# A two-layer decoder step on one core: the second feed-forward network computed by seven block products in place of eight

## The reference

```
x += 0.5 * SwiGLU_a(rms(x))
h = rms(x); p = h @ W_in;  x += W_out [ RWKV7(p_rw) | mLSTM(p_ml) | NSA(p_nsa) ]
x += MemXAttn(rms(x), mem)          # 4 heads, 256 memory tokens
x += 0.5 * SwiGLU_b(rms(x))         # D_FF = 2816

def _swiglu(h, w_up, w_down):
    gate, up = jnp.split(h @ w_up, 2, axis=-1)
    return (jax.nn.silu(gate) * up) @ w_down
```

## Time and profile before

| | us |
|---|---|
| device time, median of 3 runs | 3831.72 |
| lowest and highest of the 3 | 3829.81, 3835.63 |
| span of the profiled execution | 3827.4 |
| PE busy in it | 3565.6 (93%) |
| DVE, ACT, POOL busy | 1295.4, 564.3, 180.2 |

### The profile page before, as it was taken

The page is one execution under the profiler, slowest core; times in us unless marked ns, Lnnn a source line. Parts: engine busy times, 40 slices in busy tenths (PEclk is TensorE's granted clock), DMA queues, the critical chain, the costliest instruction groups (busy, mean ns, idle before and its releaser), DMA issues. The chain is left out here.

```text
span 3827.4 us, 44331 instructions
## 1 busy us (share of the span) xinstructions
PE 3565.6 (93%) x18084; PEld 2313.9 (60%) x18084; DVE 1295.4 (34%) x3074; ACT 564.3 (15%) x1261; POOL 180.2 (5%) x282
## 2 busy tenths in 40 slices
PE   7999899999999999997987968988899999999998
PEld 4666565666567777665665734444565556656776
DVE  3445603223312223314543458743432122111111
ACT  1000011000011101012223426630110001000000
POOL 3111100000000000000001100000000000000000
PEclk8999999999999999997687869999999999999999
DMA  6565554232234332335335431031043342233443
GB/s 158 178 190 169 169 143 117 87 97 75 88 111 118 102 98 71 101 121 112 43 82 157 141 99 55 7 124 39 12 124 91 96 119 80 76 98 110 124 128 91
DMA packets 607237, 401.76 MB, mean 105 GB/s; under 512 B 90636, under 2 KB 584060, under 8 KB 602556
## 3 DMA queue, kind: packets, MB, share of 16 engines
q1 hardware_dynamic: 578956, 314.10, 30.0%
q0 software_dynamic: 13824, 67.12, 5.6%
q10 hardware_dynamic: 14256, 17.71, 1.3%
HBM read 367.95 MB, written 36.13 MB: 106 GB/s over the span
## 5 line engine op out<-in xcount | busy, mean ns | idle before, releaser
L412 PE MATMUL psum<-arena 128*128 128x384 f32 (+1 forms) x4224 | 1335.2, 474 | 21.0 <-DVE arena L547 11.8
L412 PEld LDWEIGHTS psum<-arena 128*128 128x128 f32 x4224 | 798.8, 192 | 488.1 <-issue 25.1
L422 PE MATMUL psum<-arena 128*128 128x384 f32 (+1 forms) x2112 | 661.3, 472 | 0.0
L422 PEld LDWEIGHTS psum<-arena 128*128 128x128 f32 x2112 | 399.5, 191 | 234.9 <-issue 4.1
L445 PE MATMUL psum<-arena 128*128 128x384 f32 (+3 forms) x816 | 273.5, 492 | 6.0 <-DVE arena L547 6.0
L499 ACT ACTIVATE arena<-psum 128x384 f32<-128x384 f32 (+1 forms) x132 | 62.4, 472 | 1173.9 <-PE psum L412 1173.5
L561 DVE SCALAR_TENSOR_TENSOR arena<-arena,psum 128x384 f32<-128x384 f32 (+1 forms) x132 | 70.1, 531 | 473.6 <-ACT arena L499 472.0
L445 PEld LDWEIGHTS psum<-arena 128*128 128x128 f32 (+1 forms) x816 | 154.3, 193 | 103.7 <-issue 27.3
L570 DVE TENSOR_TENSOR arena<-psum,arena 128x384 f32<-128x384 f32 (+1 forms) x132 | 70.7, 535 | 333.4 <-PE psum L412 327.0
L577 DVE SCALAR_TENSOR_TENSOR arena<-psum,arena 128x384 f32<-128x384 f32 (+1 forms) x96 | 51.3, 535 | 362.4 <-PE psum L422 359.8
L454 PE MATMUL psum<-arena 128*128 128x264 f32 (+3 forms) x576 | 137.0, 399 | 0.0
(11 more groups left out here) (558 smaller groups left out, 3279.5 us busy)
## 6 DMA issues: line engine op xcount, KB each, us to landing
arena<-in_ffa_up SPq DMA_DIRECT2D x132, 512.0 KB, 5.2
arena<-in_ffb_up SPq DMA_DIRECT2D x132, 512.0 KB, 5.0
arena<-in_ffa_down SPq DMA_DIRECT2D x48, 704.0 KB, 4.4
arena<-in_ffb_down SPq DMA_DIRECT2D x48, 704.0 KB, 4.5
arena<-in_w_in SPq DMA_DIRECT2D x27, 1024.0 KB, 5.9
arena<-in_w_in SPq DMA_DIRECT2D x9, 1056.0 KB, 5.6
pT<-arena ACTq DMA_DIRECT2D x32, 192.0 KB, 5.4
arena<-xs SPq DMA_DIRECT2D x2, 2176.0 KB, 19.3
```

The source lines that it names most:

```text
L412: ins = mm(b[:, 0:n], w[:, g, k], hC[:, k, 0:n], start=(k == 0), stop=(k == KD - 1))
L422: ins = mm(b[:, 0:n], w[:, k], actT[:, k, 0:n], start=(k == 0), stop=(k == FH - 1))
```

## The change

The second network is computed by the Winograd form of Strassen's scheme. A product of two matrices that are each cut into 2 x 2 blocks normally takes 8 block products; the scheme takes 7, of sums and differences of the blocks, and adds the seven in several combinations. The left matrix A is a piece of weights, the right matrix B the transposed input. For an "up" tile, A has two block rows (128 gate columns, 128 up columns) and two block columns (the halves of the 1024 features, 4 matmuls each). For a "down" tile, A has the weights to two feature tiles of x, and contraction over n pairs of hidden tiles (n = 2 or 3, one of each pair in each block column). B is cut in two along the rows of the chunk as well, so each matmul now covers 192 rows (160 in chunk 2) instead of 384 (320).

The sums are S1 = A21 + A22, S2 = S1 - A11, S4 = A12 - S2, S3 = A11 - A21 on the weight side, made on POOL for each tile anew, and T1 = B12 - B11, T2 = B22 - T1, T3 = B22 - B12, T4 = B21 - T2 on the other, made on DVE once (`h_sums_dve` for the input, lines 4537 to 4540 and 4476 of the new program for the activations). The products, in the order in which PE makes them in a tile: P1 = A11 B11, P5 = S1 T1, then P4 = A22 T4 of the tile before (called "last" in the program), P6 = S2 T2, P2 = A12 B21, P3 = S4 B22, P7 = S3 T3. P1, P6, P7 and "last" add up in the same PSUM region `x_bank`, P5 and P3 in `z_bank`, P2 has `y_bank` (the other half of the bank of the tile before). In an up tile ACT copies the region after P1, P5 and P6 (`snap`), while PE goes on adding to it later; in a down tile DVE adds the region to `xT` after each product.

Tiles come in four passes in each chunk (`PASSES`): 4, 6, 6 and 6 up tiles, and after each pass 4 down tiles with n = 2, 3, 3 and 3. In all there are 66 up tiles of 7 x 4 matmuls and 48 down tiles of 7 x n.

SP loads gate and up ("lift") weights separately, 512 KB each for an up tile (384 or 256 KB for a down tile), gate weights into two buffers, lift weights into three. The gate load of tile m waits until P2 of tile m - 2 is made.

Smaller parts: `yrow` shrinks from three buffers to two; the mixer output of chunk 1 is loaded in two pieces; the norm sums of `mem_pe` for chunks 1 and 2 use bank 5, which the `mem_v` ring shares (`late_sums_pe`, `mem_bank`); `mem_dve` takes its last reciprocal itself.

```diff
+        PASSES = [(0, 2), (2, 5), (5, 8), (8, 11)]
+        FFB = []
+        for c in range(3):
+            for q, (a, z) in enumerate(PASSES):
+                FFB += [("up", c, q, f) for f in range(2 * a, 2 * z)]
+                FFB += [("down", c, q, p) for p in range(KD // 2)]
...
+        def load_gate(sp, m):
+            kind, c, q, x = FFB[m]
+            if m >= 2:
+                sp.wait_ge(products_made, PRODUCTS[m - 2, "P2"])
+                sp.wait_ge(weights_summed, GATHERS + m - 1)
...
+        def load_lift(sp, m):
+            kind, c, q, x = FFB[m]
+            if m >= 3:
+                sp.wait_ge(products_made, PRODUCTS[m - 3, "last"])
...
+        def ffb_gp(gp):
+            gp.wait_ge(out_v[2], 9 + NB + 2 * KD)
+            for m in range(len(FFB)):
+                w = left_of(m)
+                gp.wait_ge(gate_in[m % 2], GATE_0 + 16 * (m // 2 + 1))
+                gp.wait_ge(lift_in[m % 3], LIFTS_0[m % 3] + 16 * (m // 3 + 1))
+                if m >= 2:
+                    gp.wait_ge(products_made, PRODUCTS[m - 2, "P3"])
+                gp.eng.tensor_tensor(w["S1"], w["A21"], w["A22"], ALU.add).then_inc(gpsimd_done, 1)
+                gp.wait_ge(gpsimd_done, gp.done(gpsimd_done))
+                gp.eng.tensor_tensor(w["S2"], w["S1"], w["A11"], ALU.subtract).then_inc(gpsimd_done, 1)
+                gp.wait_ge(gpsimd_done, gp.done(gpsimd_done))
+                gp.eng.tensor_tensor(w["S4"], w["A12"], w["S2"], ALU.subtract).then_inc(gpsimd_done, 1)
+                gp.wait_ge(gpsimd_done, gp.done(gpsimd_done))
+                gp.eng.tensor_tensor(w["S3"], w["A11"], w["A21"], ALU.subtract).then_inc(weights_summed, 1)
+                gp.wait_ge(weights_summed, GATHERS + m + 1)
+        def product(pe, out, left, right, first=True):
+            n = left.shape[1]
+            for k in range(n):
+                ins = pe.eng.matmul(out, left[:, k], right[:, k], start=(first and k == 0), stop=(k == n - 1), skip_group_check=True)
+            ins.then_inc(products_made, 1)
+        def last_pe(pe, m):
+            pe.wait_ge(evacuated, EVACUATED[m, "u2" if FFB[m][0] == "up" else "P7"])
+            if FFB[m][0] == "up":
+                pe.wait_ge(h_summed, GATHERS + 4 * FFB[m][1] + 4)
+            else:
+                pe.wait_ge(act_summed, GATES_0 + 4 * pair_number(m) + 4)
+            product(pe, x_bank(m), left_of(m)["A22"], right_of(m)["T4"], first=False)
+        def ffb_pe(pe, c):
+            for m in range(chunk_end(c - 1) + 1, chunk_end(c) + 1):
+                A, B = left_of(m), right_of(m)
+                up, u, j = FFB[m][0] == "up", up_number(m), pair_number(m)
+                x, y, z = x_bank(m), y_bank(m), z_bank(m)
+                if m > chunk_end(c - 1) + 1:
+                    pe.wait_ge(evacuated, EVACUATED[m - 1, "g2" if FFB[m - 1][0] == "up" else "P3"])
+                else:
+                    pe.wait_ge(h_made, pe.due(h_made, KD))
+                    if m:
+                        pe.wait_ge(evacuated, EVACUATED[m - 1, "P3"])
+                pe.wait_ge(weights_summed, GATHERS + m + 1)
+                product(pe, x, A["A11"], B["B11"])
+                if starts_downs(m):
+                    last_pe(pe, m - 1)
+                    pe.wait_ge(act_summed, GATES_0 + 4 * j + 3)
+                if up:
+                    pe.wait_ge(h_summed, GATHERS + 4 * c + 3)
+                product(pe, z, A["S1"], B["T1"])
+                yield
+                if m and not starts_downs(m):
+                    last_pe(pe, m - 1)
+                if up:
+                    pe.wait_ge(snaps_made, PROJS_0 + 3 * u + 1)
+                else:
+                    pe.wait_ge(evacuated, EVACUATED[m, "P1"])
+                product(pe, x, A["S2"], B["T2"], first=False)
+                if m:
+                    pe.wait_ge(evacuated, EVACUATED[m - 1, "last"])
+                product(pe, y, A["A12"], B["B21"])
+                if up:
+                    pe.wait_ge(snaps_made, PROJS_0 + 3 * u + 2)
+                else:
+                    pe.wait_ge(evacuated, EVACUATED[m, "P5"])
+                product(pe, z, A["S4"], B["B22"], first=False)
+                if up:
+                    yield
+                    pe.wait_ge(snaps_made, PROJS_0 + 3 * u + 3)
+                else:
+                    pe.wait_ge(evacuated, EVACUATED[m, "P6"])
+                product(pe, x, A["S3"], B["T3"], first=False)
...
+                act.wait_ge(products_made, PRODUCTS[m, "P1"])
+                if before is not None:
+                    act.wait_ge(evacuated, EVACUATED[before, "a2"])
+                a.copy(snap[:, 0, 0:h], x_bank(m)).then_inc(snaps_made, 1)
+                act.wait_ge(products_made, PRODUCTS[m, "P5"])
+                a.copy(snap[:, 1, 0:h], z_bank(m)).then_inc(snaps_made, 1)
+                yield
+                act.wait_ge(products_made, PRODUCTS[m, "P6"])
+                a.copy(snap[:, 2, 0:h], x_bank(m)).then_inc(snaps_made, 1)
+                act.wait_ge(evacuated, EVACUATED[m, "g1"])
+                a.activation(tg[:, 0, 0:h], snap[:, 0, 0:h], ACT.Tanh, scale=0.5).then_inc(tanhs_made, 1)
+                act.wait_ge(evacuated, EVACUATED[m, "g2"])
+                a.activation(tg[:, 1, 0:h], snap[:, 2, 0:h], ACT.Tanh, scale=0.5).then_inc(tanhs_made, 1)
+                yield
...
+        def h_sums_dve(v, c):
...
+            v.wait_ge(h_made, v.counts[h_made.name])
+            e.tensor_tensor(t3, b22, b12, ALU.subtract).then_inc(h_summed, 1)
+            e.tensor_tensor(b12, b12, b11, ALU.subtract).then_inc(h_summed, 1)
...
+        def last_dve(v, m):
+            kind, c, q, x = FFB[m]
+            h, X = half_of(c), x_bank(m)
+            v.wait_ge(products_made, PRODUCTS[m, "last"])
+            if kind == "down":
+                to_x(v, m, "last", 1, 0, X)
+                return
+            b11, b12, b21, b22, t2, t3, t4 = act_tiles(m)
+            v.eng.tensor_tensor(b21 if x % 2 else b11, X, tg[:, 0, 0:h], ALU.mult).then_inc(evacuated, 1)
+            if x % 2:
+                v.wait_ge(evacuated, EVACUATED[m, "last"])
+                v.eng.tensor_tensor(t4, b21, t2, ALU.subtract).then_inc(act_summed, 1)
...
+        def to_x(v, m, name, row, col, src):
...
+            v.wait_ge(products_made, PRODUCTS[m, name])
+            v.eng.scalar_tensor_tensor(out=x, in0=src, scalar=0.25, in1=x, op0=ALU.mult, op1=ALU.add).then_inc(evacuated, 1)
...
+                x, y, z, u = x_bank(m), y_bank(m), z_bank(m), up_number(m)
+                if kind == "down":
+                    to_x(v, m, "P1", 0, 0, x)
+                    if i == 0:
+                        last_dve(v, m - 1)
+                    to_x(v, m, "P5", 1, 1, z)
+                    if i:
+                        last_dve(v, m - 1)
+                    to_x(v, m, "P6", 0, 1, x)
+                    v.wait_ge(evacuated, EVACUATED[m, "P1"])
+                    to_x(v, m, "P2", 0, 0, y)
+                    v.wait_ge(evacuated, EVACUATED[m, "P6"])
+                    to_x(v, m, "P3", 0, 1, z)
+                    v.wait_ge(evacuated, EVACUATED[m, "P5"])
+                    to_x(v, m, "P7", 1, 1, x)
+                    if n and q == len(PASSES) - 1:
+                        for k in range(4 * i, 4 * i + 4) if i < 2 else ():
+                            scale_one_dve(v, 4, k, xT[:, k, c0:c0 + n], hB[:, k, 0:n], n)
+                        if i == 2:
+                            h_sums_dve(v, c + 1)
+                    yield
+                    continue
+                if m:
+                    last_dve(v, m - 1)
+                yield
+                v.wait_ge(products_made, PRODUCTS[m, "P2"])
+                v.wait_ge(snaps_made, PROJS_0 + 3 * u + 1)
+                e.tensor_tensor(s1, y, s1, ALU.add).then_inc(evacuated, 1)
+                v.wait_ge(products_made, PRODUCTS[m, "P3"])
+                v.wait_ge(snaps_made, PROJS_0 + 3 * u + 3)
+                e.tensor_tensor(s2, z, s2, ALU.add).then_inc(evacuated, 1)
+                v.wait_ge(tanhs_made, PROJS_0 + 2 * u + 1)
+                v.wait_ge(evacuated, EVACUATED[m, "g1"])
+                e.scalar_tensor_tensor(out=t1, in0=t1, scalar=1.0, in1=s1, op0=ALU.add, op1=ALU.mult).then_inc(evacuated, 1)
+                v.wait_ge(products_made, PRODUCTS[m, "P7"])
+                e.tensor_tensor(s5, x, s5, ALU.add).then_inc(evacuated, 1)
+                v.wait_ge(tanhs_made, PROJS_0 + 2 * u + 2)
+                e.scalar_tensor_tensor(out=t2, in0=t2, scalar=1.0, in1=s2, op0=ALU.add, op1=ALU.mult).then_inc(evacuated, 1)
+                v.wait_ge(evacuated, EVACUATED[m, "w2"])
+                b11, b12, b21, b22, tb2, tb3, tb4 = act_tiles(m)
+                e.tensor_tensor(b22 if i % 2 else b12, s5, t2, ALU.mult).then_inc(evacuated, 1)
+                if i % 2:
+                    j = pair_number(m)
+                    v.wait_ge(evacuated, EVACUATED[m, "a2"])
```

(11 more changed lines are left out.)

361 lines of the change are left out of this document (248 added, 113 removed).

## The result

The changed kernel takes 3856.23 us, the median of 4 runs (3849.65 to 3860.84). The kernel before, run beside it, takes 3832.39 (3829.81 to 3835.63, 4 runs). The ratio is 1.0071 with a 95% interval of 1.0056 to 1.0087. So it is slower by 24 us where the forecast had 16 us faster. The time lies inside the range of 3762 to 3882 us, on the wrong side.

The account below looks back on a forecast made before the run. PE, busy 93% of the span, bounds the kernel. Terms -113 + 18 + 26 + 20 + 12 + 5 + 8 + 8 = -16 us take the 3827.4 span to 3811, forecast 3815; range 3762 to 3882 us.

Parts of the forecast that it names:

- Short waits, +8: Second network: round trips longer than a product in n = 2 down tiles (4 us), plus the stage's start; 8 us.
- Clock, +8: PE in the second network: a third of 16 waits of 3 us and more slow the clock, 1.7 us each; 8 us.
- its sign of being wrong: Forecast is wrong if the stage's PE idle and slow-clock time is under 60 us or over 140.
- PE's own work, -113: Second network's matmuls on PE: half-width streams at 0.1625 and 0.136 us cut 965 us to 852, saving 113 us.
- Rival D: Half-width matmuls on PE aren't half as long, weight loads not hidden: +88 before any wait, over 3915 us; chance 0.03.
- Weights, +18: PE waits in the second network for weight loads and POOL's sums: 18 us, of which 13 in chunk 2.
- DVE against POOL, +26, +20, +12, +5 = 63: POOL's sums delay DVE: first down tiles' P5 26 us, attention squares and scales 20, last down tiles 12, odd up tiles 5.
- Rival B: DVE becomes the bound, at SBUF-only instructions between P7 and the next tile's P2: +63 us, 3895; chance 0.25.
- Rival C: POOL becomes the bound if 512-column sums take 1.9 us beside DVE: +40 us, 3872; chance 0.12.

Follow-up runs that it names:

- no sums: Changed kernel without POOL's four weight sums per tile; PE multiplies with unsummed weights, so the output isn't the reference's: 3755.57 us, ratio 0.9819 to the kernel before.
- memsets (latency alone): Changed kernel with four POOL memsets of about equal length replacing the sums; PE waits for them and uses unsummed weights: 3799.72 us, ratio 0.9921.
- sums aside (hold alone): Changed kernel with POOL's same sums written to unread scratch; PE uses unsummed weights and waits only for loads: 3822.90 us, ratio 0.9984.
- last of the shorter sums: Changed kernel with single-sum waits, sums in 128-column pieces (256 in chunk 2), two extra attention rounds and P5's earlier wait: 3769.96 us, ratio 0.9852.

## Why the prediction was wrong

Two steps failed: "Short waits, +8" and "Clock, +8". The prediction took PE to be late almost only where POOL's sums or their hold on DVE are in the way, and the clock to fall only behind long waits. The runs show 43 us of idle time with no POOL work at all, and 31 us lost to the slow clock. The mechanism of the DVE and POOL term was right. The four kernels with and without latency and hold give the account. For each I added, over all matmuls of the stage in the trace, PE's idle time, and the time lost where the clock stood at 1.2 GHz, against 0.83 ns a column plus 2.4 ns (0.109 us at least) for each instruction:

| kernel | time | PE idle | lost to the slow clock | both, over the kernel with no sums |
|---|---|---|---|---|
| no sums | 3756 | 43 | 9 | 0 |
| memsets (latency alone) | 3800 | 73 | 19 | 40 |
| sums aside (hold alone) | 3823 | 92 | 30 | 70 |
| changed kernel | 3856 | 121 | 31 | 100 |
| last of the shorter sums | 3770 | 58 | 12 | 19 |

How a matmul at the edge of a slow stretch is counted moves up to 4 us between the two columns, and hardly their sum. The last column gives the differences of the times (44, 67, 100 and 14) within 5 us. The same count finds 10 us idle and 3 us of slow clock in the kernel before. Idle time and slow clock come to 152 us, over the 140 that the prediction had named as its sign of being wrong. Step by step:

**PE's own work, -113.** Held: 0.163 us against 0.1625. Rival D falls.

**Weights, +18.** Too low. (One reading was off without harm: 2.9 us for a load of 256 KB does not lie between 3.0 for 128 KB and 4.5 for 704; the medians after were 3.9, 3.4 and 2.9 us.) The idle time is 121 - 92 = 29; the view of waits has 30.1 in 20. Chunk 2 got 13.5 in 16 waits where 13 were predicted. The rest is in chunk 0 and 1, 9.7 of it in one wait at 2840.61, when the attention's two loads of 1 MB for its cached keys were under way, and the weight loads took 9.1 us instead of 3.9 in the median. The kernel with no sums still waits 4.6 us there for the loads alone. The prediction had no term for them; that they are the cause was not tried.

**DVE against POOL, +26, +20, +12, +5 = 63.** The mechanism held, with the strict alternation; in idle time it is 92 - 43 = 49. P5 took 18.9 of 26, the last down tiles 6.7 of 12 (2.6 of them stay with no sums). For the attention's squares and scales the size was right and the place wrong: the 20 us were looked for at "last" (line 4473), which has 4.0 in two waits, the 5 for odd up tiles included. They appear at the attention's own matmuls, which the prediction did not name: 31 us in the view of waits (lines 459, 3901, 3921, 3931, 4016) against 12 with no sums.

**Short waits, +8.** This is the term that failed most: 43 us are idle with no POOL work at all. Of these, 25 stand in the view of waits (the start of the stage 3.8, the loads 4.9, the last down tiles and the end 3.6, then the attention's 12), and 14 are gaps of under 0.2 us, too short to be seen in it; 5 to 10 us of such gaps the same count finds in the kernel before. The attention's own round trips had a cover of 5.2 us before, and the prediction counted the down tiles with n = 2 and the start of the stage only.

**Clock, +8.** This step failed outright too: 31. It priced only waits of 3 us and more, one in three. The trace has the clock at 1.2 GHz in 18 stretches of the stage, 84 us in all (with no sums in 4, 26 us; before in one, 6.8 us); one, 3.4 us long with a granted clock of 0.51, begins at 2799.60, behind a wait of 1.83 us and inside one of 1.20. In this account 22 of the 31 us hang on the hold or the latency: 9 are left without POOL.

So the sum should have been -113 + 29 + 49 + 43 + 31 = +39 by this count; the stage itself is 27 us longer (1084.8 - 1057.9). The 12 us between them are what the same count finds in the kernel before, 10 and 3. Without them the sum is +26 against the measured 27. The weights (11 too low), the short waits (35) and the clock (23) were all too low, the hold 14 too high. Either of the two large errors alone would have turned the forecast of -16 into a plus. That the time still lies in the range is partly luck: the hold was priced too high while the others were too low. Rival B named DVE as the bound at +63. Its alternation is what the traces show, and its place in part: P5 of the first down tiles waits between P7 of one tile and P2 of the next, the attention's matmuls do not. Its price is 39 us above the measured +24, and PE stays busy for 91% of the stage, so DVE is late and not the bound. Rival C falls: the 512-column sums took 1.12 to 1.30 us on the four lines, not 1.9.

## What to carry to other kernels

Before work is cut from an engine that is 100% busy, count its cover: the waits that it never had were hidden by products of 5.2 us, and here they appeared when products lasted 0.65 to 1.3 us. GpSimd sums beside DVE are worth cutting into pieces about as short as DVE's own instructions, and each consumer should wait for its own sum: these two edits, with no change in what is computed, took 3856 to 3788 us, and to 3770 with two more. While GpSimd's instructions lasted 0.7 us or more, a missed deadline on an in-order engine wasn't mended by moving the reader; the engine that was late had to be held for less time first.

## What the runs showed of the hardware

- POOL's sum holds a DVE instruction that reads SBUF only until the sum has ended: 192 columns take 0.353 us on average with no sums, 0.60 beside sums of 512 to 256 columns (0.89 on line 4538), and 1.48 at most. POOL's memsets of 0.65 to 1.2 us do not hold it at all (0.353 us beside them), and a DVE instruction with one input in PSUM is not held beside the sums (0.356 us).
- A wait of 5.81 us costs more than itself: the granted clock is 0.50 from 2772.30 to 2779.10, and of these 6.8 us PE was busy for 3.06 at half speed, another 1.5 us lost.
- The hold costs 67 us of 3823 in one kernel and 4 us (-1 to 8) in another, although POOL's sums are busy for longer there (585 us against 486) and DVE's squares are held for longer (1.17 us against 0.80).
